# Retention with the centring on ScalarE and the gates on GpSimd, and DeltaNet decay rows spread by a transfer

## The chip, the cores and the metric

The kernel runs on one core of a Trainium2 chip. The metric is the device time in microseconds, from launch to end. All arithmetic is in fp32, or in pairs of fp32r values (a rounded high part and the rest, the low part).

## The reference, cut to what matters

The trunk has two layers over 512 tokens of width 1024. Each layer is a token mixer and an MLP with squared ReLU, both between RMS norms. Layer 0 mixes by retention, layer 1 by gated DeltaNet. What the change touches:

```
def retention(h, w_in, gn_gain, w_out):            # 4 heads, q and k of 256, v of 512 columns
    ...
    scores = q k^T * decay                          # causal, per head
    o = scores v
    mu = mean(o); var = mean((o - mu)^2)            # per token and head, over 512 columns
    o = (o - mu) * rsqrt(var + EPS) * gn_gain
    y = silu(g) * o
    return y @ w_out

def gated_deltanet(...):                            # 8 heads of 128
    ...
    gc = cumsum(g)                                  # per head along the tokens
    decay = where(causal, exp(gc[i] - gc[j]), 0)    # per head and chunk
    lower = where(strict, (k beta) k^T * decay, 0)
    ...
```

The kernel works in chunks of 128 tokens, so DeltaNet has 32 units (8 heads by 4 chunks), each with one triangle of decays, 128 by 128.

## The kernel before, in words

**Engines and streams.** Every engine has its own program, written out by hand, and they meet at counting semaphores. SyncE streams the weights from memory in chunks of 1 MB into two buffers (`w_raw`). ScalarE rounds each chunk to its high part (L940, two instructions), GpSimd subtracts to get the low part (L310, two instructions), and TensorE may use the chunk when `w_ready` says so. A projection is made of parts: one chunk of weights by one of four output tiles, twelve matmuls in three kinds (L417 to L419). A PSUM bank is 128 by 512; there are eight, and a group of parts fills four of them. Banks are released by the semaphore `emptied`.

**Retention** (TensorE L576, VectorE L1545 to L1578, ScalarE L1105 to L1124). TensorE first does the scores of head 0 (L585, 16 instructions in the profile, into banks 0 to 3), then for each head the scores of the next one and then scores by values (L599, 20 instructions in the profile for ten matmuls, into banks 4 to 7). VectorE multiplies the scores by the decay table (L1550); the table is loaded by a transfer that ScalarE issues after its last gate (L1105). TensorE waits for all four decayed tiles of a head at once. For each of the 16 tiles (four heads by four token tiles) VectorE then takes mean and variance (L1566, L1567), subtracts the mean and multiplies by the gate in one instruction that reads the bank (L1570) and releases it, and makes 1/sqrt with one Newton step (L1409 to L1414) from ScalarE's root (L1112). ScalarE scales the tile (L1118). Only behind all that TensorE transposes the first eight tiles (L613, four transposes a tile), ScalarE takes the high parts (L1123) for all tiles, VectorE the low parts (L1577), and the output projection begins (`group` with `RET_OUT`, its first part reads tile 0, 1, 2, 3 of head 0, and it waits for all four at once). The other eight tiles are transposed inside that projection.

**DeltaNet gate rows.** The decays' cumulative sums come from two small matmuls with a triangle of ones and with ones (`sum_g`, L687, L688), for all 32 units as columns. The triangle of decays also needs the sums along the other axis, as a row that all partitions hold. `row_sums` (L695) makes it on TensorE: for each unit, a matmul of the column, broadcast to 128 by 128, with the triangle of ones, into PSUM. `triangles` does this for two heads at a time, together with the products of k with itself (L701), at four places inside the projections of v and q. ScalarE takes the exponential from PSUM with a bias per partition (L1225) into `attn`, GpSimd puts zeros above the diagonal (L366), and VectorE multiplies (L1712), which TensorE waits for before the next pair. At the places around it ScalarE squares k (L1214), starts the convolutions (L1198) and rounds weights, and VectorE convolves (L1670) and makes the columns for k (L1682 on).

Of the kernel before, what the change touches and what calls it, by code (L numbers as in the profile page):

```python
# [79 lines left out]
def hybrid_trunk(nc, x, norm_gains, ret_w_in, ret_gn_gain, ret_w_out, gdn_w_in, gdn_conv_w, gdn_a_log,  # L80
# [42 lines left out]
    bn = plan.tile("bn", [P, RH * TT, 16], F32, act_at + 24 * KB)  # L123
    BN_MEAN, BN_VAR, BN_ROOT, BN_NEWTON, BN_RSTD = 6, 7, 8, 9, 12
# [41 lines left out]
    head_rows = big("head_rows", [P, 4, GH], F32, 99.25)  # L166
    ct = plan.tile("ct", [P, 16, UNITS], F32, dump_at)
# [39 lines left out]
    with ExitStack() as ctx:  # L207
# [94 lines left out]
        def _(pool):  # L302
# [39 lines left out]
            low_parts(4, FIRST_CHUNK[1] - 2)  # L342
# [71 lines left out]
        def _(pe):  # L414
# [161 lines left out]
            def retention():  # L576
                pe.wait_ge(emptied, 4 * RET_OUT[0])
                pe.wait_ge(sem("roped"), KT)

                def scores(h):  # L580
                    if h:
                        pe.wait_ge(sem("decayed"), TT * h)
                    for i in range(TT):
                        for d in range(2):
                            done = pe.matmul(bank[i][:, 0:T - i * P], qk_t[:, KT + 2 * h + d, i * P:(i + 1) * P],  # L585
                                             qk_t[:, 2 * h + d, i * P:T], start=d == 0, stop=d == 1)
                        done.then_inc(sem("scored"), 1)

                scores(0)
                for h in range(RH):  # L590
                    if h + 1 < RH:
                        scores(h + 1)
                    else:
                        pe.wait_ge(sem("decayed"), TT * RH)
# [7 lines left out]
                turn_y(0, 8)  # L602

            def turn_y(first, last):

                for n in range(first, last):
                    h, m = n // TT, n % TT
                    pe.wait_ge(sem("y_scaled"), n + 1)
                    pe.wait_ge(sem("y_gated"), min(n + 9, RH * TT))
# [5 lines left out]
                    done.then_inc(sem("y_transposed"), 1)  # L615

# [66 lines left out]
            def sum_g():  # L683
# [4 lines left out]
                pe.matmul(bank[7][:, UNITS:2 * UNITS], ones, col[:, G, :], start=True, stop=True)\  # L688
                    .then_inc(sem("g_summed"), 1)

            def row_sums(h, b):

                for n in range(TT):
                    g = col[:, G, h * TT + n:h * TT + n + 1].broadcast_to([P, P])
                    done = pe.matmul(bank[b][:, n * P:(n + 1) * P], g, tri, start=True, stop=True)  # L695
                return done
# [15 lines left out]
            def triangles(first):  # L712
# [5 lines left out]
                for i in range(2):  # L718
# [3 lines left out]
                    row_sums(first + i, b).then_inc(sem("tri_rows"), 1)  # L722
# [199 lines left out]
            group(RET_OUT[1], 0, 4, False, y_hi, y_lo, {(0, 1): lambda: turn_y(8, 12), (0, 3): lambda: turn_y(12, 16)},  # L922
                  tiles=(sem("y_low"), 0))
# [10 lines left out]
        def _(act):  # L934
# [173 lines left out]
            splits(RET_OUT, 0, 4, last=1)  # L1108
            for n in range(RH * TT + 1):
                if n < RH * TT:  # L1110
                    act.wait_ge(sem("varied"), n + 1)
                    act.activation(bn[:, n, BN_ROOT:BN_ROOT + 1], bn[:, n, BN_VAR:BN_VAR + 1], ACT.Sqrt, bias=eps)\  # L1112
                        .then_inc(sem("gn_rooted"), 1)
                if n:
                    h, m = (n - 1) // TT, (n - 1) % TT
                    act.wait_ge(sem("gn_inverted"), n)
                    y = gate[:, m, h * RV:(h + 1) * RV]
                    act.activation(y, y, ACT.Copy, scale=bn[:, n - 1, BN_RSTD:BN_RSTD + 1])\  # L1118
                        .then_inc(sem("y_scaled"), 1)
            for n in range(RH * TT):  # L1120
                h, m = n // TT, n % TT
                act.wait_ge(sem("y_transposed"), n + 1)
                act.activation(y_hi[:, 4 * h:4 * h + 4, m * P:(m + 1) * P], tall(y_bank(n)), ACT.Copy)\  # L1123
                    .then_inc(sem("y_high"), 1)  # L1124
# [94 lines left out]
            def tri_exps(first):  # L1219
                for h in (first, first + 1):  # L1220
                    act.wait_ge(sem("tri_rows"), h + 1)
                    b = (0 if h < 4 else 4) + 2 * (h % 2)
                    for n in range(TT):
                        u = h * TT + n
                        done = act.activation(attn[:, u, :], bank[b][:, n * P:(n + 1) * P], ACT.Exp,  # L1225
# [22 lines left out]
            for gi in range(8):  # L1248
# [50 lines left out]
                if gi == 2:  # L1299
                    square_heads(4, GH)  # L1300
# [101 lines left out]
        def _(dve):  # L1402
# [3 lines left out]
            def inv_root(x, root, temp, out_, scale=1.0, add=EPS):  # L1406
# [4 lines left out]
                if x.shape[-1] == 1:  # L1411
                    link(dve.tensor_scalar(t[2], t[0], t[1], t[1], ALU.mult, ALU.mult))
                    link(dve.tensor_scalar(t[2], t[2], -0.5, 1.5, ALU.mult, ALU.add))
# [139 lines left out]
            def inverted(n):  # L1553
                dve.wait_ge(sem("gn_rooted"), n + 1)
                inv_root(bn[:, n, BN_VAR:BN_VAR + 1], bn[:, n, BN_ROOT:BN_ROOT + 1],
                         lambda t: bn[:, n, BN_NEWTON + t:BN_NEWTON + t + 1], bn[:, n, BN_RSTD:BN_RSTD + 1])\
                    .then_inc(sem("gn_inverted"), 1)

            decayed(0)
            for h in range(RH):  # L1560
                if h + 1 < RH:
                    decayed(h + 1)
                for m in range(TT):
                    n = TT * h + m
                    dve.wait_ge(sem("attended"), n + 1)
                    link(dve.bn_stats(bn[:, n, 0:6], bank[4 + m][:, :]))  # L1566
                    dve.bn_aggr(bn[:, n, BN_MEAN:BN_VAR + 1], bn[:, n, 0:6]).then_inc(sem("varied"), 1)  # L1567
                    dve.wait_ge(sem("varied"), n + 1)
                    y = gate[:, m, h * RV:(h + 1) * RV]
                    dve.scalar_tensor_tensor(y, bank[4 + m][:, :], bn[:, n, BN_MEAN:BN_MEAN + 1], y,  # L1570
# [322 lines left out]
```

## Time and profile before

| | |
|---|---|
| median of 3 runs | 1518.33 us (1517.52 to 1521.31) |
| the profiled execution | 1518.14 us |
| its span, first to last instruction | 1516.2 us |
| mean granted TensorE clock | 0.996 of full speed |
| retention, first score matmul to first matmul of the output projection | 285.91 to 347.50 us |
| DeltaNet, where row sums are made | 892.61 to 937.0 us |

The times of instructions in the profile are counted from the span's start. What lies around the span is 1.9 us. An engine's busy time matters only where another engine waits for it; the chain that ended last says which engine the end hangs on.

### The profile page before, as it was taken

To read this page: it belongs to the slowest core of one execution; us is meant where nothing else is said; L and a number is where in the kernel's file an instruction comes from. 1 tells how busy PE (TensorE), PEld (TensorE's weight loads), DVE (VectorE), ACT (ScalarE), POOL (GpSimd) and SP (SyncE) were. 2 spreads that over 40 slices of the span, in tenths; PEclk is the share of its full clock that TensorE was granted. 3 is DMA by queue.
4 is the path that set the end of the run, shared out by engine and by line. 5 is a ranking of instruction groups with operands and counts; after the bars stand their busy time and mean duration, and the time that the engine had idled before them with its cause. 6 is when DMAs were issued, how large, how long until landed. Compare 5 with 4: busy or idle time off the path is not lost.

```text
span 1516.2 us, 19636 instructions
## 1 busy us (share of the span) xinstructions
PE 1471.4 (97%) x7657; PEld 1245.3 (82%) x7657; DVE 607.9 (40%) x1121; ACT 550.7 (36%) x1046; POOL 629.4 (42%) x283
## 2 busy tenths in 40 slices
PE   6999999998999999999999999999998999999997
PEld 6988888657889888888889978889988988888886
DVE  3641002383265410134045544995747540024223
ACT  5232333233253222232234576655735222223231
POOL 5244443302544444444445243355336253534441
PEclk9999999999999999999999999999999999999999
DMA  6222323400333232322323112211023223232321
GB/s 237 102 84 86 108 83 111 139 0 29 98 99 112 84 111 83 96 99 85 110 84 119 56 56 84 84 56 56 15 70 101 81 84 111 83 97 98 111 84 56
DMA packets 66507, 134.22 MB, mean 89 GB/s; under 512 B 3616, under 2 KB 4096, under 8 KB 66176
## 3 DMA queue, kind: packets, MB, share of 16 engines
q1 hardware_dynamic: 64016, 125.90, 25.4%
q10 hardware_dynamic: 2416, 7.27, 1.4%
q8 instruction: 53, 0.87, 0.2%
q14 instruction: 22, 0.18, 0.0%
HBM read 131.06 MB, written 2.10 MB: 88 GB/s over the span
## 4 chain that ended last, share of the span: by engine, by line
PE 88%; DVE 5%; ACT 3%; POOL 2%; DMA 1%; issue 1%; SPq 0%; ACTq 0%; DVEq 0%
PE bank L417 26%; PE bank L418 26%; PE bank L419 26%; PE bank L599 2%; POOL side_lo L310 1%; PE bank L792 1%; PE bank L805 1%; PE bank L585 1%; PE bank L701 1%; ACT squares L1214 1%; DVE mix L1458 1%; DMA w_raw<-in_ret_w_in_dram 1%; DVE act_lo L1484 1%; DVE gv L1670 1%; POOL w_lo L310 1%
## 5 line engine op out<-in xcount | busy, mean ns | idle before, releaser
L310 POOL TENSOR_TENSOR w_lo<-w_raw,w_hi 128x1024 fp32r<-128x1024 f32 (+1 forms) x218 | 520.4, 2410 | 741.0 <-ACT w_hi L940 740.9
L940 ACT ACTIVATE w_hi<-w_raw 128x1024 fp32r<-128x1024 f32 x210 | 211.0, 1055 | 466.7 <-PE bank L419 422.0
L417 PE MATMUL bank<-act_hi,w_hi 128*128 128x512 f32 (+1 forms) x832 | 300.0, 361 | 8.5 <-DVE act_lo L1484 7.3
L418 PE MATMUL bank<-act_lo,w_hi 128*128 128x512 f32 (+1 forms) x832 | 298.3, 359 | 0.0
L419 PE MATMUL bank<-act_hi,w_lo 128*128 128x512 f32 (+1 forms) x832 | 298.3, 359 | 0.0
L418 PE MATMUL bank<-w_lo,hid_hi 128*128 128x512 f32 x480 | 189.0, 394 | 0.0
L417 PE MATMUL bank<-w_hi,hid_hi 128*128 128x512 f32 x480 | 188.2, 392 | 0.0
L419 PE MATMUL bank<-w_hi,hid_lo 128*128 128x512 f32 x480 | 186.4, 388 | 0.0
L417 PEld LDWEIGHTS bank<-act_hi,w_hi 128*128 128x128 f32 x832 | 158.8, 191 | 32.9 <-DVE act_lo L1484 8.8
L1589 DVE TENSOR_TENSOR relu_sq<-relu 128x512 f32<-128x512 f32 x64 | 48.8, 763 | 328.4 <-ACT relu L963 328.1
L419 PEld LDWEIGHTS bank<-act_hi,w_lo 128*128 128x128 f32 x832 | 158.6, 191 | 22.6
L418 PEld LDWEIGHTS bank<-act_lo,w_hi 128*128 128x128 f32 x832 | 158.8, 191 | 21.9
L417 PE MATMUL bank<-w_hi,act_hi 128*128 128x512 f32 x320 | 125.0, 391 | 1.5 <-issue 1.1
L419 PE MATMUL bank<-w_hi,act_lo 128*128 128x512 f32 x320 | 124.5, 389 | 0.0
L418 PE MATMUL bank<-w_lo,act_hi 128*128 128x512 f32 x320 | 124.5, 389 | 0.0
L417 PEld LDWEIGHTS bank<-w_hi,hid_hi 128*128 128x128 f32 x480 | 90.1, 188 | 20.9
L419 PEld LDWEIGHTS bank<-w_hi,hid_lo 128*128 128x128 f32 x480 | 90.1, 188 | 20.2
L418 PEld LDWEIGHTS bank<-w_lo,hid_hi 128*128 128x128 f32 x480 | 90.2, 188 | 18.1
L1540 DVE TENSOR_TENSOR gate<-gate,gains x16 | 16.9, 1072 | 149.8 <-ACT gate L963 149.8
L417 PE MATMUL bank<-act_hi,side_hi 128*128 128x256 f32 x256 | 72.4, 283 | 1.4 <-POOL side_lo L310 1.4
L417 PEld LDWEIGHTS bank<-w_hi,act_hi 128*128 128x128 f32 x320 | 60.1, 188 | 15.0 <-issue 1.9
L418 PE MATMUL bank<-act_lo,side_hi 128*128 128x256 f32 x256 | 71.4, 279 | 0.0
(258 smaller groups left out, 2150.4 us busy)
## 6 DMA issues: line engine op xcount, KB each, us to landing
w_raw<-in_mlp_w_up_dram SPq DMA_DIRECT2D x32, 1024.0 KB, 5.4
w_raw<-in_mlp_w_down_dram SPq DMA_DIRECT2D x32, 1024.0 KB, 5.0
w_raw<-in_ret_w_in_dram SPq DMA_DIRECT2D x24, 1024.0 KB, 5.1
w_raw<-in_gdn_w_in_dram SPq DMA_DIRECT2D x16, 1024.0 KB, 5.3
w_raw<-in_ret_w_out_dram SPq DMA_DIRECT2D x8, 1024.0 KB, 4.9
gains<-in_norm_gains_dram ACTq DMA_DIRECT2D x8, 512.0 KB, 6.1
w_raw<-in_gdn_w_out_dram SPq DMA_DIRECT2D x4, 1024.0 KB, 5.1
resid<-in_x_dram SPq DMA_DIRECT2D x4, 512.0 KB, 9.2
```

The source lines that it names most:

```text
L310: done = nc.gpsimd.tensor_tensor(LO[slot][:, kt, :], w_raw[:, raw, kt, :], HI[slot][:, kt, :].bitcast(F32), ALU.subtract)
L417: pe.matmul(dst, sta_hi, mov_hi, start=first, stop=False)
L418: pe.matmul(dst, sta_hi, mov_lo, start=False, stop=False)
L419: return pe.matmul(dst, sta_lo, mov_hi, start=False, stop=last)
L585: done = pe.matmul(bank[i][:, 0:T - i * P], qk_t[:, KT + 2 * h + d, i * P:(i + 1) * P], qk_t[:, 2 * h + d, i * P:T], start=d == 0, stop=d ...
L599: done = pe.matmul(bank[4 + j][:, :], score[:, h % 2, i, j * P:(j + 1) * P], v_tm[:, i, h * RV:(h + 1) * RV], start=i == 0, stop=i == j)
L701: done = pe.matmul(bank[b][:, n * P:(n + 1) * P], gk[:, h, n * P:(n + 1) * P], other[:, h, n * P:(n + 1) * P], start=True, stop=True)
L792: done = pe.matmul(bank[r][:, n * P:(n + 1) * P], neg_l_t[:, u, :], inv[:, u - batch * UNITS // 2, :], start=True, stop=True)
L805: done = pe.matmul(bank[4 + r][:, n * P:(n + 1) * P], half_prod[:, u - batch * UNITS // 2, :], inv_t[:, u, :], start=True, stop=True)
L940: act.activation(HI[raw if slot is None else slot][:, kt, :], w_raw[:, raw, kt, :], ACT.Copy)\
L1540: dve.tensor_tensor(g, g, gains[:, :, :].rearrange("p a n -> p (a n)")[:, bass.ds(i * GC, GC)], ALU.mult).then_inc(sem("gate_gained"), 1)
L1589: dve.tensor_tensor(relu_sq[:, m, :], relu[:, m, :], relu[:, m, :], ALU.mult)\
```

## The change

**Retention.** `centre` on ScalarE now takes the root, and then reads the bank and writes mean minus value to a new buffer `centred` of three tiles (an Identity activation with scale -1 and the mean as bias); this releases the bank. GpSimd multiplies that tile with the gate (16 multiplications between two loops of low parts). VectorE's instruction L1570 is gone; its Newton step turns the sign. `scale_y` is as before, behind GpSimd. TensorE waits tile by tile for decayed scores, starts the scores of head 0 once banks 0 to 3 are free, transposes tiles 0 to 3 in the middle of head 3 and tiles 4 and 5 behind it, and `first_ret_out` waits for each tile of the low part by itself and transposes the last ten tiles between its parts. ScalarE and VectorE take the first high and low parts before their last tile of statistics.

**DeltaNet.** `row_sums` is gone. `sum_g` has a third matmul that gives the sums with units as rows, 32 by 128. ScalarE copies it to SBUF, sends it to memory (16 KB), waits for that transfer just before it squares the last four heads of k, and issues a second one that reads it back into `attn` for all 128 partitions (2 MB). The exponentials then read and write `attn`.

```diff
@@ tensor, retention
-                pe.wait_ge(emptied, 4 * RET_OUT[0])
+                pe.wait_ge(emptied, 4 * (RET_OUT[0] - 1))
 def scores(h):
-    if h:
-        pe.wait_ge(sem("decayed"), TT * h)
     for i in range(TT):
+        if h:
+            pe.wait_ge(sem("decayed"), TT * (h - 1) + i + 1)
...
     for j in range(TT):
+        pe.wait_ge(sem("decayed"), TT * h + j + 1)
         if h:
-            pe.wait_ge(sem("y_gated"), TT * (h - 1) + j + 1)
+            pe.wait_ge(sem("y_centred"), TT * (h - 1) + j + 1)
...
+        if h == RH - 1 and j == 1:
+            pe.wait_ge(sem("decayed"), TT * RH)
+            turn_y(0, 4)
-turn_y(0, 8)
+turn_y(4, 6)
+def first_ret_out():
+    turns = {(0, 0): (6, 8), (0, 2): (8, 12), (1, 0): (12, 16)}
+    for j in range(4):
+        for m in range(TT):
+            pe.wait_ge(sem("y_low"), TT * j + m + 1)
+            done = part(RET_OUT[1], j, 0, 4, m, False, y_hi, y_lo, fresh=m == 0)
...
@@ gpsimd
-            low_parts(4, FIRST_CHUNK[1] - 2)
+            low_parts(4, RET_OUT[1] + 2)
+            for n in range(RH * TT):
+                pool.wait_ge(sem("y_centred"), n + 1)
+                y = gate[:, m, h * RV:(h + 1) * RV]
+                nc.gpsimd.tensor_tensor(y, y, centred[:, n % 3, :], ALU.mult).then_inc(sem("y_gated"), 1)
+            low_parts(RET_OUT[1] + 2, FIRST_CHUNK[1] - 2)
@@ scalar
+def centre(n):
+    act.wait_ge(sem("varied"), n + 1)
+    act.activation(root <- var, ACT.Sqrt)
+    if n >= 3:
+        act.wait_ge(sem("y_gated"), n - 2)
+    act.activation(centred[:, n % 3, :], bank[4 + n % TT][:, :], ACT.Identity, scale=-1.0,
+                   bias=bn[:, n, BN_MEAN:BN_MEAN + 1]).then_inc(sem("y_centred"), 1)
 for n in range(RH * TT + 1):
     if n < RH * TT:
+        centre(n)
     if n:
+        scale_y(n - 1)
+    if n == RH * TT - 2:
+        high_y(0, 4)
+high_y(4, RH * TT)
@@ vector
     dve.wait_ge(sem("attended"), n + 1)
+    if n == RH * TT - 1:
+        low_y(0, 1)
     link(dve.bn_stats(...)); dve.bn_aggr(...).then_inc(sem("varied"), 1)
-    dve.scalar_tensor_tensor(y, bank[4 + m][:, :], mean, y, ALU.subtract, ALU.mult)
     inverted(n)
+low_y(1, RH * TT)
@@ DeltaNet: tensor
+                pe.matmul(bank[7][0:UNITS, P:2 * P], col[:, G, :], tri, start=True, stop=True)
-                    row_sums(first + i, b).then_inc(sem("tri_rows"), 1)
@@ DeltaNet: scalar, before and in group 2
+  act.activation(g_rows[:, :], bank[7][0:UNITS, P:2 * P], ACT.Copy).then_inc(sem("g_rows_out"), 1)
   act.activation(EXP_G ...); act.activation(EXP_TOT ...)
+  act.wait_ge(sem("g_rows_out"), 1)
+  act.dma_start(g_spread, g_rows[:, :]).then_inc(sem("g_kept"), 16)
   act.wait_ge(sem("rest_made"), 1); act.activation(ct[:, 8, :] ...)
+  act.wait_ge(sem("g_kept"), 16)
+  act.dma_start(attn as 128 x 4096, g_spread broadcast to 128 partitions).then_inc(sem("g_spread"), 16)
   square_heads(4, GH)
@@ tri_exps
-  act.wait_ge(sem("tri_rows"), h + 1)
+  act.wait_ge(sem("g_spread"), 16)
-  act.activation(attn[:, u, :], bank[b][:, n * P:(n + 1) * P], ACT.Exp, bias=...)
+  act.activation(attn[:, u, :], attn[:, u, :], ACT.Exp, bias=...)
```

## Rows read from the trace of the kernel before

**Rows 1.** The page, part 4: the chain that ended last, by engine.

```profile
PE 88%; DVE 5%; ACT 3%; POOL 2%; DMA 1%; issue 1%; SPq 0%; ACTq 0%; DVEq 0%
```

**Rows 2.** Timeline of TensorE, retention: start, us, line, count [idle before, releaser].

```profile
285.91 4.58 PE L585 MATMUL bank<-qk_t 128*128 128x512 f32 x16 [0.78 <-ACT gate L963]
292.16 4.58 PE L585 MATMUL bank<-qk_t 128*128 128x512 f32 x16 [1.67 <-DVE score L1550]
...
347.50 0.80 PE L417 MATMUL bank<-w_hi,y_hi 128*128 128x512 f32 x1 [3.91 <-DVE y_lo L1577]
...
354.53 1.91 PE L613 MATMUL bank<-square,gate 128*128 128x128 f32 x16
...
361.79 1.91 PE L613 MATMUL bank<-square,gate 128*128 128x128 f32 x16
```

**Rows 3.** Busy time by window (us, engines, granted clock PEclk), start of output projection.

```profile
347.50:350.70 3.20, 3.20 (x8) 2.55 (x9) 2.34 (x4) 0.84 (x2) 0.00 (x0) 0.52 0.00 0
```

**Rows 4.** The chain that ended last in order of time, retention: start, us, what.

```profile
285.41 4.94 DMA decay<-in_decay_dram
290.43 1.70 DVE score L1550 x4
...
322.55 8.60 PE bank L599 x20
...
354.69 1.75 PE bank L613 x16
```

**Rows 5.** Timeline of VectorE, one of the 16 retention tiles and the next.

```profile
325.94 0.69 DVE L1566 BATCH_NORM_STATS2 bn<-bank 128x6 f32<-128x512 f32 x1
...
326.88 0.75 DVE L1570 SCALAR_TENSOR_TENSOR gate<-bank,bn,gate 128x512 f32<-128x512 f32 x1
...
328.43 0.69 DVE L1566 BATCH_NORM_STATS2 bn<-bank 128x6 f32<-128x512 f32 x1
```

**Rows 6.** Timeline of ScalarE, retention.

```profile
289.67 1.28 ACT L1112 ACT_TABLE_LOAD   x1
...
344.35 3.99 ACT L1123 ACTIVATE y_hi<-bank 128x512 fp32r<-128x512 f32 x8
```

**Rows 7.** Instructions that touch gains, GpSimd: duration in ns, min/median/max.

```profile
L337 POOL TENSOR_TENSOR normed<-resid,gains x8: 1272/1314/1321, 6.5 to 1139.8; 128x512 f32<-128x512 f32 x8
```

**Rows 8.** Timeline of TensorE, DeltaNet projections.

```profile
884.32 0.47 PE L417 MATMUL bank<-act_hi,w_hi 128*128 128x512 f32 x1 [0.75 <-issue]
...
892.61 1.05 PE L695 MATMUL bank<-square,col 128*128 128x128 f32 x8
...
905.28 1.16 PE L695 MATMUL bank<-square,col 128*128 128x128 f32 x8 [0.69 <-DVE neg_l_t L1712]
...
954.40 1.97 PE L651 MATMUL bank<-square,gv 128*128 128x128 f32 x16
```

**Rows 9.** The chain that ended last, DeltaNet: row sums of one head.

```profile
922.75 0.89 PE bank L695 x8
```

**Rows 10.** Timeline of ScalarE, DeltaNet.

```profile
876.97 0.23 ACT L1296 ACTIVATE ct<-ct 128x32 f32<-128x32 f32 x1 [0.54 <-DVEq L1679]
879.55 0.28 ACT L1214 ACTIVATE squares<-bank 128x128 bf16<-128x128 f32 x1 [2.35 <-PE bank L651]
...
894.15 0.23 ACT L1318 ACTIVATE ct<-ct 128x32 f32<-128x32 f32 x1 [6.17 <-DVEq L1685]
```

**Rows 11.** Timelines of GpSimd and of VectorE, DeltaNet.

```profile
895.40 4.75 POOL L310 TENSOR_TENSOR w_lo<-w_raw,w_hi 128x1024 fp32r<-128x1024 f32 x2 [16.68 <-ACT w_hi L940]
...
945.35 8.99 DVE L1670 SCALAR_TENSOR_TENSOR gq<-bank,conv_w,gq 128x509 f32<-128x509 f32 x12 [5.04 <-ACT gq L1198]
```

**Rows 12.** DMA issues: count, KB each, us from issue to landing.

```profile
out_dram<-resid SPq DMA_DIRECT2D x8, 256.0 KB, 2.0
gains<-in_ret_gn_gain_dram ACTq DMA_DIRECT2D x1, 1024.0 KB, 4.6
...
head_rows<-in_gdn_dt_bias_dram ACTq DMA_DIRECT2D x1, 4.0 KB, 4.9
```

More of the change, by code:

```diff
@@ L615, in turn_y @@
                     done.then_inc(sem("y_transposed"), 1)
+            def first_ret_out():
[4 more added lines that the diff above has]
+                        done = part(RET_OUT[1], j, 0, 4, m, False, y_hi, y_lo, fresh=m == 0)
+                        if j == 3:
+                            done.then_inc(bank_full, 1)
+                        elif m == 3:
+                            done.then_inc(chunk_used, 1)
+                        if (j, m) in turns:
+                            turn_y(*turns[j, m])
             def mlp(layer):
@@ L687, in sum_g @@
                 pe.matmul(bank[7][:, 0:UNITS], tri, col[:, G, :], start=True, stop=True)
-                pe.matmul(bank[7][:, UNITS:2 * UNITS], ones, col[:, G, :], start=True, stop=True)\
+                pe.matmul(bank[7][:, UNITS:2 * UNITS], ones, col[:, G, :], start=True, stop=True)
+                pe.matmul(bank[7][0:UNITS, P:2 * P], col[:, G, :], tri, start=True, stop=True)\
                     .then_inc(sem("g_summed"), 1)
[L691 to L696, printed above, removed]
             def products(h, b, other):
@@ L920, in _ @@
             retention()
-            group(RET_OUT[1], 0, 4, False, y_hi, y_lo, {(0, 1): lambda: turn_y(8, 12), (0, 3): lambda: turn_y(12, 16)},
-                  tiles=(sem("y_low"), 0))
+            first_ret_out()
             tail(1, RET_OUT, y_hi, y_lo)
@@ new lines, in scale_y, with high_y @@
+            def scale_y(n):
+                h, m = n // TT, n % TT
+                act.wait_ge(sem("gn_inverted"), n + 1)
+                act.wait_ge(sem("y_gated"), n + 1)
+                y = gate[:, m, h * RV:(h + 1) * RV]
+                act.activation(y, y, ACT.Copy, scale=bn[:, n, BN_RSTD:BN_RSTD + 1]).then_inc(sem("y_scaled"), 1)
+            def high_y(first, last):
+                for n in range(first, last):
+                    h, m = n // TT, n % TT
+                    act.wait_ge(sem("y_transposed"), n + 1)
+                    act.activation(y_hi[:, 4 * h:4 * h + 4, m * P:(m + 1) * P], tall(y_bank(n)), ACT.Copy)\
+                        .then_inc(sem("y_high"), 1)
@@ L1118, in _ @@
[L1118 to L1124, printed above, removed]
+                    scale_y(n - 1)
+                if n == RH * TT - 2:
+                    high_y(0, 4)
@@ L1220, in tri_exps @@
                 for h in (first, first + 1):
[L1221 to L1222 removed]
+                    act.wait_ge(sem("g_spread"), 16)
                     for n in range(TT):
                         u = h * TT + n
[L1225 removed]
+                        done = act.activation(attn[:, u, :], attn[:, u, :], ACT.Exp,
                                               bias=col[:, NEG_GCUM, u:u + 1])
@@ L1404, in _, with inv_root @@
             link = chain.link
-            def inv_root(x, root, temp, out_, scale=1.0, add=EPS):
+            def inv_root(x, root, temp, out_, scale=1.0, add=EPS, sign=1):
                 t = [temp(n) for n in range(3)]
@@ L1555, in inverted, with low_y @@
                 inv_root(bn[:, n, BN_VAR:BN_VAR + 1], bn[:, n, BN_ROOT:BN_ROOT + 1],
-                         lambda t: bn[:, n, BN_NEWTON + t:BN_NEWTON + t + 1], bn[:, n, BN_RSTD:BN_RSTD + 1])\
+                         lambda t: bn[:, n, BN_NEWTON + t:BN_NEWTON + t + 1], bn[:, n, BN_RSTD:BN_RSTD + 1], sign=-1)\
                     .then_inc(sem("gn_inverted"), 1)
+            def low_y(first, last):
+                for n in range(first, last):
+                    h, m = n // TT, n % TT
+                    dve.wait_ge(sem("y_high"), n + 1)
+                    where = (slice(None), slice(4 * h, 4 * h + 4), slice(m * P, (m + 1) * P))
+                    dve.tensor_tensor(y_lo[where], tall(y_bank(n)), y_hi[where].bitcast(F32), ALU.subtract)\
+                        .then_inc(sem("y_low"), 1)
             decayed(0)
```

32 lines of the change are left out of this document (12 added, 20 removed).

## The prediction

> **What bounds the kernel now.** I read the chain that ended last first. TensorE carries 88% of it [rows 1], so a microsecond is won only where TensorE idles, runs at the low clock, or does work that goes away. I then went along TensorE's timeline through the two stages that the change touches and, at each idle stretch, to the timeline of the engine that ended it.
>
> In retention TensorE idles three times. The first idle is 0.78 us ahead of the first scores; the second is 1.67 us, ended by decayed scores at 292.16 [rows 2]. These hang on a transfer: the decay table is issued at 285.41, takes 4.94 us, and VectorE starts at 290.43 and needs 1.70 us for four tiles, for all of which TensorE waits [rows 4]. From there to the last matmul of head 3 TensorE is full: heads 2 and 3 begin at 322.55 and take 8.60 us each [rows 4], to 339.75. VectorE however needs 2.49 us a tile (325.94 to 328.43 [rows 5]), and ends its sixteenth late; behind it come scaling, high parts and low parts. So the third idle stretch: eight tiles of transposes (twice the 1.75 us of 16 [rows 4]) would end at 343.25, and the output projection starts at 347.50 [rows 2]. It also starts slowly: in the window that begins there the granted clock is 0.52, that is 1.2 of 2.4 GHz [rows 3], after an idle stretch of 3.91 us. The first two parts take 354.53 - 347.50 = 7.03 us, where the next two take 361.79 - 354.53 - 1.75 = 5.51 us [rows 2, 4].
>
> In the DeltaNet projections TensorE is nearly full, with 0.75 us idle at 884.32 and 0.69 us at 905.28 [rows 8]. A second chain runs beside it, close behind: squares of k from 879.55, convolution, the root at 894.15 for which ScalarE had waited 6.17 us [rows 10], the weight rounding behind that in ScalarE's queue, and GpSimd's low part from 895.40 to 900.15 [rows 11].
>
> **Retention, step by step.** Starting the scores of head 0 earlier (up to 0.78 us) is worth nothing: TensorE then waits for the decay table that much longer, and the table's issue is not moved. Waiting per tile is worth something: the first decayed tile is 512 wide and comes some 0.7 us (an estimate from the 0.69 us that a 512-wide read of a bank takes VectorE [rows 5]) after 290.43, so TensorE resumes at 291.1 and not at 292.16: **1.0 us**. The three later tiles are there before TensorE asks.
>
> VectorE loses 0.75 us a tile [rows 5], but then waits for ScalarE's root, which that instruction had covered, so I take 2.2 us a tile. Four tiles and four decayed tiles are then some 10.6 us a head against TensorE's 12.9 (8.60 and about 4.3 for scores [rows 2, 4]). ScalarE gets 16 centrings: about 0.5 us each, as the eight reads of a bank in 3.99 us [rows 6]; with root and scaling some 1.4 us a tile. GpSimd gets 16 products of 1.3 us [rows 7]. It has nothing else there, since its low parts of the first two output chunks are put ahead. Neither is near the 3.2 us a tile that TensorE takes (12.9 / 4). A bank is asked for one head after it was filled, so the longer way to its release costs nothing. That cover is four to nine microseconds wide at each tile; if it were gone, each late tile would cost what it is late.
>
> At the end: head 3 starts at 331.15 - 1.0 = 330.1. Its parts of 1, 2, 3 and 4 matmuls (0.86 us each) with four tiles of transposes (1.75 us) after the second end at 331.0, 332.7, 337.1 and 340.5; two more tiles of transposes end at 341.4. The first low part is made at 340.5 + 0.7 = 341.2, because VectorE does it before its last statistics and ScalarE took its high part by about 340. So the output projection can start at once, with 0.2 us to spare. The last tile's way is statistics 342.1, centring 343.0, product 344.3, scaling 345.0; the banks for tiles 6 and 7 are wanted at 344.2 (centring of tile 15 done at 343.0), the low parts of the second head at 350.5 (there by about 348). The third chunk of output weights is rounded behind the last high part on ScalarE, so it moves forward with TensorE; before and after it is ready some 4 us ahead. So the wait of 347.50 - 343.25 = **4.2 us** goes, and with it the slow start, 7.03 - 5.51 = **1.5 us**. The transposes are only moved. Retention: 1.0 + 4.2 + 1.5 = **6.7 us**. What is next late is the first low part; if it comes 1 us later, 1 us of this is lost. I bound the stage from 3 us (it starts idle, with half of the slow start left) to 7.5 us (the first idle goes too).
>
> **DeltaNet, step by step.** Each head's row sums take 0.89 us on TensorE [rows 9], in eight heads 7.1 us. The added matmul has the same width as one of the four units in such a row: 0.2 us. Not all of this lies on the path:
> - The first pair (892.61 [rows 8]) is worth nothing. TensorE gets to the next weight chunk 1.8 us earlier, but its low part is ready at 900.15 whatever TensorE does [rows 11], and the next products wait for the masked triangles of the first pair, whose exponentials ScalarE reaches in its queue only behind the rounding, not behind TensorE. The idle 0.69 us at 905.28 [rows 8] grows instead.
> - The second pair comes at that place and is worth its 1.8 us, since what is behind it is TensorE's own work.
> - The third and fourth are worth 3.6 us. ScalarE does not wait for row sums there any more, so VectorE's triangles, the diagonal and the next convolution begin some 6 us earlier. Before, that convolution ran from 945.35 to 954.34 [rows 11] and TensorE's transposes at 954.40 [rows 8] came right behind it. After, I have it end at 948.4 and TensorE there at 949.3.
> - The 0.2 us of the added matmul shift the squares and with them the whole chain.
>
> So 1.8 + 3.6 - 0.2 = **5.2 us**. I take 5.1, for the slightly longer way through the copy.
>
> **The two transfers.** ScalarE issues the store at about 876.7, after the copy (0.2 us). The nearest rows are the stores at the end, 2.0 us for 256 KB, and the smallest load, 4.9 us for 4 KB issued amid others [rows 12]. I take 2.0, because it is a store on idle queues. Landing at 878.7 and 0.4 us of issue end at 879.1, inside the 2.35 us that ScalarE idles before 879.55 [rows 10]. Cover gone (4.9 us), the squares start at 882.0, **2.2 us** late, and all behind them. The lower end is nothing, not a gain, as the idle stretch hangs on TensorE. Behind the waiting instruction stand the squares, for which TensorE waits (884.32 [rows 8]). The spread of 2 MB: 1 MB broadcast took 4.6 us [rows 12], so some 7 to 10 us with a weight chunk beside it, landing by 889. It is wanted by ScalarE at 901, the weight chunk at 894.15.
>
> The Trainium skill (DMA: Bandwidth & Descriptors, Anatomy of one DMA) gives about 2.0 us fixed and bytes at 436 GB/s, and warns that the receipt of a write can be surprisingly long when the target is HBM. By its fit the store would take 2.0 us and the spread 6.8 us, as in my sum; by its warning it speaks for the rival below.
>
> **Sum.** 6.7 + 5.1 = 11.8 us from the profiled execution's 1518.14 us (span 1516.2 and 1.9 around it): **1506.3 us**. The median of the runs is 1518.33, so the two agree to 0.2 us.
>
> **Rivals.**
> - *The store is slow* (12%). For it: the 4.9 us row. Against it: the 2.0 us rows and empty queues. 2.2 us lost: 1508.5.
> - *The second chain sets DeltaNet* (10%). For it: the idle stretches at 884.32 and 905.28. Against it: its later waits went through the row sums themselves. TensorE then waits for the 5.1 us that it no longer works: 1511.4.
> - *The start of the output projection stays late* (8%). For it: only 0.2 us to spare, and three engines in a row. It costs 3.7 us: 1510.
> - *Table loads take the place of the wait* (4%), the slower side. ScalarE's table load takes 1.28 us [rows 6]. One load served all roots and copies before, but no row shows an Identity. If it needed another table than the root, each tile would have two loads, 2.56 us, so about 3.9 us a tile against TensorE's 3.2. Counted from 298, the fifteenth ends at 356.5 and the projection starts at 357.8, 10.3 us later than before; less 5.1 of DeltaNet that is 1523.3. It decides from 3.2 us a tile, and turns the sum to a loss from about 3.6.
> - Anything else, either way (6%).
>
> The Trainium skill (ScalarE: Activation LUTs, Table sets) says that copy and identity are in every set. By it the last rival has no loads; the case's rows show it for copy alone.
>
> **Chances.** Forecast 60%, with a range of its own of 1504.5 to 1508. The range reaches down to 1502.5 (the upper bound of retention, 7.5, and all 7 us of row sums come to 14.5, less what I can't rule out) and up to 1511.5, which takes in the three faster rivals and leaves out table loads and half of the rest. A measurement here can tell about 0.3%, 4.6 us. All cases but the table loads and part of the rest are faster by more than that: 0.91 faster, 0.05 within, 0.04 slower.
>
> **What would show it.** Right: no TensorE idle between 291 and the end of the first output group; granted clock 1.00 at its start; one table load in the stage; group of the output projection starting at 341 to 342; TensorE idle growing to about 1 us before the second pair of products and no other new one; turning of v at 949 less 6.7, that is near 942.6 on the new time scale; a store of 2 us. Wrong: ScalarE waiting over 2.5 us before the squares of the fifth head, TensorE idle ahead of the output projection, or the exponentials waiting for the spread.

## The result, and the profile after

The changed kernel takes 1505.62 us (median of 4 runs, 1504.56 to 1506.10) against 1517.92 (4 runs beside it, 1517.42 to 1521.31): ratio 0.9915, 95% interval 0.9903 to 0.9928, 12.3 us less. 1506.3 had been forecast. One further execution of the kernel before, beside later runs, took 3017.77 us and is left out of every comparison.

The page, part 4 (by engine), answers [rows 1]:

```profile
PE 90%; DVE 4%; ACT 2%; POOL 1%; DMA 1%; issue 1%; SPq 0%; ACTq 0%; DVEq 0%
```

The timeline of TensorE in retention answers [rows 2] (start, us, engine, line, count, idle before and releaser). Scores are now L594, scores by values L608, transposes L626, the projection L426:

```profile
283.77 4.48 PE L594 MATMUL bank<-qk_t 128*128 128x512 f32 x16
289.98 4.58 PE L594 MATMUL bank<-qk_t 128*128 128x512 f32 x16 [1.74 <-DVE score L1592]
...
331.36 1.91 PE L626 MATMUL bank<-square,gate 128*128 128x128 f32 x16
333.11 6.17 PE L608 MATMUL bank<-v_tm,score 128*128 128x512 f32 x14
339.12 1.04 PE L626 MATMUL bank<-square,gate 128*128 128x128 f32 x8
340.07 0.51 PE L426 MATMUL bank<-w_hi,y_hi 128*128 128x512 f32 x1
342.95 1.03 PE L626 MATMUL bank<-square,gate 128*128 128x128 f32 x8
```

The first idle stretch is gone and the second has grown into its place: 1.74 us, ended by the first decayed tile. From 289.98 to the end of the projection there is none. The projection starts at 340.07 and its first part takes its 2.9 us at once, at full clock (busy time by window, the last columns being granted clock, DMA share and GB/s; it answers [rows 3]):

```profile
340.07:343.40 3.33, 3.33 (x18) 2.76 (x18) 2.83 (x10) 1.86 (x5) 1.31 (x1) 1.00 0.00 0
```

The chain that ended last, in order of time, at the second scores, answers [rows 4]; one tile of 0.70 us is waited for where it was four:

```profile
284.20 4.95 DMA decay<-in_decay_dram
...
289.24 0.70 DVE score L1592
...
289.98 4.58 PE bank L594 x16
```

One retention tile on VectorE (two starts of its statistics), ScalarE and GpSimd, and ScalarE's table load (timelines; these answer [rows 5 to 7]):

```profile
288.46 1.28 ACT L1131 ACT_TABLE_LOAD   x1
...
323.43 0.69 DVE L1619 BATCH_NORM_STATS2 bn<-bank 128x6 f32<-128x512 f32 x1
...
325.58 0.69 DVE L1619 BATCH_NORM_STATS2 bn<-bank 128x6 f32<-128x512 f32 x1
...
324.57 0.67 ACT L1135 ACTIVATE centred<-bank,bn 128x512 f32<-128x512 f32 x1
...
325.31 1.27 POOL L350 TENSOR_TENSOR gate<-gate,centred 128x512 f32<-128x512 f32 x1 [0.89 <-ACT centred L1135]
```

VectorE takes 2.15 us a tile (323.43 to 325.58) where it took 2.49; the centring takes ScalarE 0.67 us and the product GpSimd 1.27, both beside it. There is one table load in the stage, so Identity shares the root's table. The Trainium skill (ScalarE: Activation LUTs, Table sets) says that identity is in every set, and the trace agrees (one load, 1.28 us). VectorE at the end of head 3: the first low part, then the last statistics:

```profile
339.32 0.69 DVE L1607 TENSOR_TENSOR y_lo<-bank,y_hi 128x512 fp32r<-128x512 f32 x1 [1.18 <-ACT y_hi L1151]
339.93 0.69 DVE L1619 BATCH_NORM_STATS2 bn<-bank 128x6 f32<-128x512 f32 x1
```

The low part ends at 340.01, and the projection starts at 340.07: the narrow place is narrower than forecast (0.06 us to spare and not 0.2), and holds.

In DeltaNet, TensorE (answers [rows 8]; L678 transposes, which is called turning below, the products of k are L722, the added matmul L716):

```profile
859.11 1.91 PE L678 MATMUL bank<-square,gk 128*128 128x128 f32 x16
...
865.08 0.41 PE L716 MATMUL bank<-square,col 128*32 128x128 f32 x2
865.41 0.50 PE L426 MATMUL bank<-act_hi,w_hi 128*128 128x512 f32 x1
...
886.08 1.16 PE L722 MATMUL bank<-gk 128*128 128x128 f32 x8 [0.37 <-DVE gv L1714]
...
892.25 0.50 PE L426 MATMUL bank<-act_hi,w_hi 128*128 128x512 f32 x1 [0.69 <-POOL w_lo L313]
897.59 2.05 PE L722 MATMUL bank<-gk 128*128 128x128 f32 x16 [0.96 <-DVE neg_l_t L1756]
...
941.22 1.91 PE L678 MATMUL bank<-square,gv 128*128 128x128 f32 x16
```

The idle stretches of 0.37 us (ahead of the second products of the first pair) and 0.69 us (at the low part of the next weight chunk) are new: they take up 1.06 us of the first pair's removed 1.8. The third, 0.96 us ahead of the second pair, is the 0.69 us of the kernel before [rows 8], grown by 0.27. From 897.59 to the turning of v at 941.22 there is none. ScalarE (answers [rows 10]): both transfers are issued without holding it up, and the squares wait for TensorE as before:

```profile
866.62 0.34 ACTq L1333 DMA_DIRECT2D g_spread<-g_rows  x1
...
868.74 0.34 ACTq L1340 DMA_DIRECT2D attn<-g_spread  x1
871.62 0.28 ACT L1251 ACTIVATE squares<-bank 128x128 bf16<-128x128 f32 x1 [2.66 <-PE bank L678]
...
893.15 2.45 ACT L1261 ACTIVATE attn<-attn,col 128x128 f32<-128x128 f32 x8
```

The same eight exponentials, read from PSUM, in the kernel before:

```profile
901.10 2.18 ACT L1225 ACTIVATE attn<-bank,col 128x128 f32<-128x128 f32 x8
```

The store landed in 1.4 us and the spread in 7.8 (answers [rows 12]), over 16 us before the exponentials.

**Where the time went.** Profiled executions differ in where retention begins, by 1.7 us among these kernels (the decay table is issued between 283.81 and 285.54), so stretches between marks are compared, not clock readings. Marks: the issue of the decay table; the start of the scores of head 1 (the second scores); the first transposes of the norm behind retention; the first turning of k; the turning of v. The medians come from several groups of runs, in which the kernel before took 1517.9 to 1519.4 us, so medians of different groups compare only to some 1.5 us.

| kernel | issue to 2nd scores | issue to norm | k to v | median us |
|---|---|---|---|---|
| before | 6.75 | 149.54 | 86.91 | 1517.92 |
| changed | 5.78 | 142.83 | 82.11 | 1505.62 |
| retention alone | 5.78 | 142.82 | 86.95 | 1510.62 |
| DeltaNet alone | 6.86 | 149.68 | 82.14 | 1513.88 |
| waits only | 5.57 | 148.52 | 86.91 | 1517.25 |
| late turns | 5.81 | 148.14 | 82.13 | 1512.89 |
| four stores | 5.76 | 142.78 | 87.02 | 1510.11 |
| first pair kept | 5.78 | 142.83 | 82.11 | 1506.24 |
| last pairs kept | 5.80 | 142.85 | 85.73 | 1510.39 |
| root behind | 5.82 | 142.84 | 80.31 | 1504.82 |
| order only | 5.89 | 144.64 | 82.14 | 1506.34 |
| root behind, first pair kept | 5.62 | 142.67 | 80.86 | 1504.56 |
| decay early | | 140.81 | 82.14 | 1504.83 |
| both early | | 140.77 | 80.27 | 1501.79 |

(With the decay table early the scores of heads 0 and 1 run as one piece, so the first column is empty.)

Retention gives 149.54 - 142.83 = 6.71 us; DeltaNet 86.91 - 82.11 = 4.80 up to the turning of v, and 5.22 up to the joining of the inverses, the matmuls that put the inverted triangles together (from the first turning of k at 867.49 to 1027.49 before, 859.11 to 1013.89 after). The last 0.42 us are no steady part of the gain. From the turning of v to the joining the kernel before takes 73.09 us, and of the eleven executions with the changed DeltaNet six take 73.0 and five 72.7. Where it is 73.0, TensorE idles some 0.4 us at a low part on the way; where it is 72.7, as in the changed kernel, that stretch is missing. The kernel before has it:

```profile
997.78 0.50 PE L417 MATMUL bank<-w_hi,act_hi 128*128 128x512 f32 x1 [0.41 <-POOL w_lo L310]
```

The profiled pair differs by 13.4 us in its spans: 6.71 and 5.22, 1.2 ahead of the issue of the decay table, where kernels that are equal up to there differ as much, and 0.3 elsewhere. So 11.5 to 11.9 us are traced to the change, and the medians say 12.3.

### The profile page after: what moved, and what is told of

It is laid out like the page before. It is cut to its first block, busy times and chain, and to the rows that moved or that the text cites. A ratio compares the mean times of both kernels' runs of the same rounds, so it can differ in the third digit from the quotient of the medians.

```text
span 1502.8 us, 19558 instructions
## 1 busy us (share of the span) xinstructions
PE 1461.3 (97%) x7595; PEld 1235.9 (82%) x7595; DVE 598.6 (40%) x1105; ACT 560.5 (37%) x1063; POOL 649.2 (43%) x299
## 4 chain that ended last, share of the span: by engine, by line
PE 90%; DVE 4%; ACT 2%; POOL 1%; DMA 1%; issue 1%; SPq 0%; ACTq 0%; DVEq 0%
PE bank L426 27%; PE bank L427 27%; PE bank L428 26%; PE bank L608 2%; POOL side_lo L313 1%; PE bank L812 1%; PE bank L825 1%; PE bank L678 1%; PE bank L594 1%; PE bank L722 1%; DVE mix L1500 1%; DMA w_raw<-in_ret_w_in_dram 1%; DVE act_lo L1526 1%; DVE gv L1714 1%; PE bank L473 1%
## 5 line engine op out<-in xcount | busy, mean ns | idle before, releaser
L426 PE MATMUL bank<-act_hi,w_hi 128*128 128x512 f32 (+1 forms) x832 | 299.7, 360 | 9.8 <-DVE act_lo L1526 7.9
L426 PE MATMUL bank<-w_hi,hid_hi 128*128 128x512 f32 x480 | 188.2, 392 | 0.0
L426 PEld LDWEIGHTS bank<-act_hi,w_hi 128*128 128x128 f32 x832 | 158.3, 190 | 34.8 <-DVE act_lo L1526 9.2
L426 PE MATMUL bank<-w_hi,act_hi 128*128 128x512 f32 x320 | 124.9, 390 | 1.0 <-issue 1.0
L426 PEld LDWEIGHTS bank<-w_hi,hid_hi 128*128 128x128 f32 x480 | 90.1, 188 | 20.9
L426 PE MATMUL bank<-act_hi,side_hi 128*128 128x256 f32 x256 | 72.3, 282 | 1.4 <-POOL side_lo L313 1.4
L982 ACT ACTIVATE relu<-bank 128x512 f32<-128x512 f32 x64 | 38.0, 597 | 91.2 <-PE bank L428 91.2
L426 PEld LDWEIGHTS bank<-w_hi,act_hi 128*128 128x128 f32 x320 | 60.1, 188 | 14.3 <-issue 1.8
```

The source lines that it names most:

```text
L426: pe.matmul(dst, sta_hi, mov_hi, start=first, stop=False)
L982: act.activation(dst, bank[4 * p + m][:, :], func).then_inc(emptied, 1)
```

## The experiments

**Retention alone and DeltaNet alone.** The hunks of the one part on the kernel before.

> The retention part of the change alone, DeltaNet as before. My theory: it is worth 6.7 us by itself (from 1517.9 to about 1511.2), all of it won before the second part of the output projection. Rival: the two parts are not independent, and the whole 12.3 us needs both; then this one moves by 4 us or less or by 9 us or more.

> The DeltaNet part alone, retention as before. Theory: 4.8 to 5.1 us (to about 1513.0), though 7.1 us of row sums are gone: none from the first pair of heads. Rival (the second chain of ScalarE and VectorE sets the stage): under 1 us, 1517. Rival (all row sums were on the path): 6.9 us, 1511.0.

Measured: 1510.62 us, ratio 0.9945 (0.9929 to 0.9962), and 1513.88 us, ratio 0.9968 (0.9956 to 0.9981). The medians say 7.6 and 4.3 us against 1518.20 beside them, the stretches 6.72 and 4.77: independent, and they sum to the whole (11.5 us by the stretches, 11.9 by these medians).

**Waits only.**

```diff
 def scores(h):
-    if h:
-        pe.wait_ge(sem("decayed"), TT * h)
     for i in range(TT):
+        if h:
+            pe.wait_ge(sem("decayed"), TT * (h - 1) + i + 1)
```

The per-tile wait ahead of scores by values, and the early start of the first scores, are in it too.

> The kernel before with only TensorE's waits per decayed tile and the early start of the scores; centring, gates, transposes as before. Theory: the scores of head 1 start 1.0 to 1.1 us earlier and everything moves by that: 1516.9. The earlier scores of head 0 (0.78 us) are lost in the wait for the decay table: TensorE idles 1.7 us ahead of the second scores still. Rival: both idle stretches are won, 2.4 us, 1515.5. Rival: VectorE, which was nearly full, takes it back, 1517.9.

Measured: 1517.25 us, ratio 0.9991 (0.9982 to 1.0001), too little for the total to tell. The stretch from the issue of the table to the norm is 1.02 us shorter, and TensorE idles 1.53 us ahead of the second scores (timeline of TensorE):

```profile
289.56 4.58 PE L585 MATMUL bank<-qk_t 128*128 128x512 f32 x16 [1.53 <-DVE score L1550]
...
344.89 0.50 PE L417 MATMUL bank<-w_hi,y_hi 128*128 128x512 f32 x1 [3.92 <-DVE y_lo L1577]
```

The wait ahead of the projection is unmoved, 3.92 us.

**Late turns.**

```diff
-                        if h == RH - 1 and j == 1:
...
-                            turn_y(0, 4)
-                turn_y(4, 6)
+                turn_y(0, 8)
...
-            first_ret_out()
+            group(RET_OUT[1], 0, 4, False, y_hi, y_lo, {(0, 1): turn_y(8, 12), (0, 3): turn_y(12, 16)}, ...)
```

High and low parts are taken behind the last tile again, as before.

> The changed kernel, with the transposes and the start of the output projection in the old order (eight tiles of transposes behind the last head, all four low parts waited for, high and low parts behind the last tile). Centring on ScalarE and gates on GpSimd stay. Theory: the wait for the first low parts hangs on the order, not on VectorE's load: the way of the last tile over ScalarE and GpSimd is as long as VectorE's lag was, so TensorE idles some 3.6 us and starts at the low clock again: 5.1 us slower than the changed kernel, 1510.7. Rival: the 0.75 us a tile off VectorE brought most of the gain, then at most 2 us slower, 1507.6.

Measured: 1512.89 us, ratio to the kernel before 0.9964 (0.9951 to 0.9976), 7.3 us over the changed kernel's median. The stage is 5.31 us longer than the changed one; this is the effect of the edit. Another 1.6 us of the profiled execution come from the clock at the joining of the inverses (below), where nothing was edited; whether the other executions had this is not shown. TensorE idles 3.62 us and then has 0.57 of its clock (timeline, and busy time by window):

```profile
344.36 0.50 PE L426 MATMUL bank<-w_hi,y_hi 128*128 128x512 f32 x1 [3.62 <-DVE y_lo L1604]
```

```profile
344.30:348.10 3.80, 3.74 (x10) 2.94 (x11) 2.40 (x5) 0.90 (x2) 0.00 (x0) 0.57 0.00 0
```

With VectorE's load taken off and the old order, nearly all of the gain at that place is gone: 148.14 us to the norm, against 148.52 with the waits alone. That raised the reverse question.

**Order only.** Centring and gates back on VectorE (and TensorE's waits for a free bank back on `y_gated`):

```diff
-                act.activation(centred[:, n % 3, :], bank[4 + n % TT][:, :], ACT.Identity, scale=-1.0, ...)
...
-                nc.gpsimd.tensor_tensor(y, y, centred[:, n % 3, :], ALU.mult).then_inc(sem("y_gated"), 1)
+                    dve.scalar_tensor_tensor(y, bank[4 + m][:, :], mean, y,
+                                             ALU.subtract, ALU.mult).then_inc(sem("y_gated"), 1)
```

> The changed kernel with the centring and the gates back on VectorE in one instruction, as in the kernel before (nothing on GpSimd, only the root and the scaling on ScalarE). The new order stays: waits per tile, transposes in the middle of head 3, first high and low part ahead of the last tile, output projection tile by tile; DeltaNet as changed. Theory, formed after the late turns came out 5.3 us slower in the stage: the order alone brings the gain. VectorE ends the fifteenth tile some 0.7 us before the last bank is filled, so the first low part is late by 0.3 us at most: within 0.5 us of the changed kernel, 1505.6 to 1506.1. Rival: VectorE's 2.49 us a tile are needed back, it lags at the end as before, and at least 2.5 us of the 6.7 go: 1508.1 or more.

Measured: 1506.34 us, ratio 0.9925 (0.9907 to 0.9944), 0.7 us over the changed kernel's median. The stretch is 1.81 us longer, and the timeline shows where: the second scores take 6.28 us and not 4.58, at a granted clock of 0.56, behind an idle stretch of 1.85 us (1.74 in the changed kernel, where the clock stayed at 1.00). That the edit caused this is not shown. From the third scores on it is the same, 305.07 to 429.12 us (124.05) against 302.99 to 427.03 (124.04), with no idle ahead of the projection:

```profile
290.37 6.28 PE L588 MATMUL bank<-qk_t 128*128 128x512 f32 x16 [1.85 <-DVE score L1582]
...
341.20 1.04 PE L620 MATMUL bank<-square,gate 128*128 128x128 f32 x8
342.15 0.51 PE L420 MATMUL bank<-w_hi,y_hi 128*128 128x512 f32 x1
```

```profile
290.30:293.90 3.60, 3.53 (x5) 1.59 (x6) 1.04 (x5) 0.00 (x0) 2.20 (x1) 0.56 0.77 227
```

So moving the centring to ScalarE and the gates to GpSimd gives nothing that this kernel shows; the new order gives all. VectorE ends the fifteenth tile in time (it idles 0.29 us behind it), and the low part of the first is taken before the sixteenth in either. Apart from the wait for each decayed tile, which was run alone above, the new order has several parts: the transposes in the middle of head 3, the high and low parts ahead of the last tile, and a wait for each low part by itself. Which of them are needed was not tested.

**Four stores.**

```diff
+                    for again in range(1, 4):
+                        act.wait_ge(sem("g_kept"), 16 * again)
+                        act.dma_start(g_spread, g_rows[:, :]).then_inc(sem("g_kept"), 16)
-                    act.wait_ge(sem("g_kept"), 16)
+                    act.wait_ge(sem("g_kept"), 64)
```

> The changed kernel with three more stores of the same 16 KB, each waited for before the next, ahead of the spread. In the changed kernel a store lands in 1.4 us, the spread is issued at 868.74 and the squares of k start at 871.62, so 2.5 us (2.88 less the 0.34 us of issue) are free there. Theory: the wait lies in ScalarE's idle time and is paid only beyond it: three more stores of about 1.5 us move the issue to 873.2, the squares to 873.6, 2.0 us late, and the turning of v by as much: 1507.6. Rival: the waits are on the path in full, 4.5 us later, 1510.1. Rival: the squares are not on the path, no change, 1505.6.

Measured: 1510.11 us (2 runs), ratio 0.9942 (0.992 to 0.9963). ScalarE:

```profile
869.00 3.13 ACTq L1341 DMA_DIRECT2D g_spread<-g_rows  x3
876.35 0.34 ACTq L1343 DMA_DIRECT2D attn<-g_spread  x1
876.75 0.28 ACT L1251 ACTIVATE squares<-bank 128x128 bf16<-128x128 f32 x1 [7.53 <-DMA g_spread<-g_rows]
```

Three more stores took 7.35 us and not 4.5: the last was issued by 871.8 (869.00 + 3.13 less 0.34 of issue), behind a weight chunk of 1 MB issued at 870.75, and landed some 4.5 us later. The one before it, issued at about 870.4 and so just ahead of the chunk, still took 1.4. Of the 7.35 us the 2.5 free ones are hidden, and 4.9 reach the turning of v (87.02 against 82.11). So the size of my theory failed by the price of a store, and its total fell on the rival's by chance; that idle time hides the wait, and that the squares are on the path, stand. It also gives the change's risk a number, from one case: the same 16 KB cost 1.4 us on idle queues and once some 4.5 behind a weight chunk (that the chunk is the cause is argued from the times of issue), and in the changed kernel the chunk is issued 3.9 us behind the store.

**First pair kept, last pairs kept.** The row sums computed again for heads 0 and 1, or 4 to 7, with no reader:

```diff
+                    if first == 0:        # or: first >= 4
+                        row_sums(first + i, b)
                     products(first + i, b + 1, gk)
```

> The changed kernel with the row sums of the first two heads computed again (1.8 us of TensorE's work, nobody reads them). Theory: the first pair is worth nothing, since TensorE waits behind it for the low part of the next weight chunk and for the masked triangles; 1505.6, TensorE's idle stretch of 0.69 us at that low part and the 0.37 us ahead of the second products gone, the stretch from the first turning of k to the turning of v 82.1 us as before. Rival (each microsecond of TensorE's work counts): 1507.4.

> The changed kernel with the row sums of the last four heads computed again (3.6 us of TensorE's work, nobody reads them). Theory: these lie on the path in full, 3.6 us slower, 1509.2; the stretch from the first turning of k to the turning of v is 85.7 us. Rival (ScalarE and VectorE set this stage): under 1 us, 1506.4.

Measured: 1506.24 us, 0.9918 (0.9900 to 0.9936), and 1510.39 us, 0.9943 (0.9925 to 0.9960). The stretch from k to v is 82.11, to the hundredth that of the changed kernel, and 85.73, which is 3.62 more. (The median of the second is 4.8 us higher; its profiled execution has the low clock at the joining, of which below.) Of TensorE in the first:

```profile
887.79 1.06 PE L728 MATMUL bank<-gk 128*128 128x128 f32 x8
888.60 0.48 PE L426 MATMUL bank<-act_hi,w_hi 128*128 128x512 f32 x1
892.80 0.41 PE L426 MATMUL bank<-act_hi,w_hi 128*128 128x512 f32 x1
898.05 2.05 PE L728 MATMUL bank<-gk 128*128 128x128 f32 x16 [0.98 <-DVE neg_l_t L1764]
```

The idle 0.37 and 0.69 us are filled, and the 0.98 stays (0.96 in the changed kernel). That is 1.06 us of the 1.78 us put back; the other 0.7 lie in no idle stretch that the profile names.

**Root behind, and with the first pair kept.**

```diff
+                if gi == 3:                      # behind the rounding of group 3
+                    act.wait_ge(sem("kq_x_made"), 1)
+                    act.activation(ct[:, 2, :], ct[:, 0, :], ACT.Sqrt).then_inc(sem("kq_rooted"), 1)
...
-                if gi == 2:                      # end of group 2
-                    act.wait_ge(sem("kq_x_made"), 1)
-                    act.activation(ct[:, 2, :], ct[:, 0, :], ACT.Sqrt).then_inc(sem("kq_rooted"), 1)
```

> The changed kernel, and ScalarE takes the root for the columns of k behind the rounding of the next weight chunk and not ahead of it. In the changed kernel ScalarE idles 6.17 us for VectorE there, rounds behind it, and GpSimd's low part is late by 0.69 us, blocks two VectorE column instructions (2.29 and 2.31 us) and the exponentials come 2 us later; TensorE idles 0.37, 0.69 and 0.96 us. Theory: with the rounding ahead, the low part is ready some 6 us earlier and the masked triangles some 2 to 4 us earlier, so 0.69 and 0.96 us go: 1.6 us faster, 1504.0, and the first pair's row sums have then paid. Rival: the squares, the convolution and the products' bank set that place anyway: no change.

> The kernel with the root behind the rounding, and the row sums of the first two heads computed again. Theory: with the low part early the place is no longer bound by it, so TensorE's 1.8 us count here, where they cost nothing in the changed kernel: the stretch from the first turning of k to the turning of v is 82.1 us, not the 80.3 of the kernel with the root behind; 1506.6. Rival: the first pair is hidden here as well, 80.3 us, 1504.8.

Measured: 1504.82 us, 0.9905 (0.9887 to 0.9923), stretch 80.31, 1.80 less; and 1504.56 us (2 runs), 0.9911 (0.9891 to 0.9931), stretch 80.86. The totals of the two lie too close to tell them apart; the stretches do. GpSimd's low part starts 20.7 us behind the first turning of k, where it was 28.4, and VectorE's two column instructions that ran beside it take 0.19 us each and not 2.29 and 2.31. GpSimd and TensorE with the root behind:

```profile
881.69 4.77 POOL L313 TENSOR_TENSOR w_lo<-w_raw,w_hi 128x1024 fp32r<-128x1024 f32 x2 [9.48 <-ACT w_hi L959]
...
888.01 1.16 PE L722 MATMUL bank<-gk 128*128 128x128 f32 x8 [0.37 <-DVE gv L1714]
...
897.62 2.05 PE L722 MATMUL bank<-gk 128*128 128x128 f32 x16 [0.25 <-DVE neg_l_t L1756]
```

The first theory holds: the rounding in ScalarE's queue bound the place (1.80 us by the stretch, 1.6 expected). The second does not: with the low part early, the first pair's 1.8 us cost only 0.55. Row sums fill the 0.37 us in which TensorE waits for VectorE's convolution to release a bank and the 0.25 us for the masked triangles. These account for half of the 1.2 us that are hidden; where the rest goes is not shown.

**Decay early, both early.** The table of head 0 is loaded into `decay_0` (the place of `dump`) at the start; VectorE waits for the large table only at head 1.

```diff
+    decay_0 = plan.tile("decay_0", [P, T], F32, dump_at)
...
+            act.dma_start(decay_0[:, :], decay_c[:, 0, :]).then_inc(sem("decay_0_landed"), 16)
```

> The changed kernel, with the decay table of head 0 loaded a second time at the start into a buffer that is free until then. Theory: TensorE's 1.74 us idle ahead of the scores of head 1 hang on the table's transfer alone, and with it the early start of the scores pays too: no idle there, 1.7 us faster, 1503.9. Rival: VectorE, which has the last gate products before it, or the banks hold it up in the same place: under 0.5 us.

> Both: the root behind the rounding, and the decay table of head 0 early. Theory: two places of TensorE's own path, so the sum, 1.8 + 1.7 = 3.5 us faster than the changed kernel, 1502.1, and 16 us faster than the kernel before. Rival: one of them is given back at the next wait, 1503.9.

Measured: 1504.83 us, 0.9912 (0.9895 to 0.9929), and 1501.79 us (4 runs, 1500.19 to 1504.06), 0.9896 (0.9878 to 0.9914). In the first all 32 score instructions of heads 0 and 1 run without a pause, and the stretch to the norm is 2.02 us shorter, the 1.74 and the restart:

```profile
284.00 8.79 PE L595 MATMUL bank<-qk_t 128*128 128x512 f32 x32
```

Its total is only 0.8 us lower. The profiled execution has the low clock at the joining; whether the other three had it, and what else keeps the total up, is not shown. With both, 1.84 us less from k to v and 2.06 to the norm, 3.9 by the stretches and 3.8 by the medians: 16.4 us less than the kernel before beside it. (Its four runs spread over 3.9 us, so the medians' 3.8 is a rough number.) This is the best version run.

## Why the prediction was right, and where it was not

- *The decay wait, 1.0 us.* 0.97 measured, and the early scores of head 0 gave nothing, as forecast (1.74 us idle in their place). Loading the table early shows what held them.
- *The late start of the projection, 4.2 us, and the slow clock, 1.5.* 6.71 less 0.97 is 5.74, forecast 5.7. But the cause that I put first, that VectorE needs 2.49 us a tile and so ends late, was not what had to be mended: with VectorE as loaded as before, the order alone won the same. What counted was that everything stood behind the sixteenth tile, though it was wanted for the first. I had bounded VectorE's time per tile and worked out its new end; I did not work out its old load under the new order, which would have shown this (fifteenth tile done before the last bank is filled).
- *0.2 us to spare at the first low part.* It was there 0.06 us ahead of TensorE's start. The start itself, 340.07, is 341.3 on the scale of the kernel before (retention begins 1.2 us earlier in this execution), inside the forecast 341 to 342.
- *DeltaNet.* The split in pairs was right: 0, 1.8 and 3.6 forecast, 0.00 and 3.62 measured for first and last. The second was not put back by itself; by subtraction, 4.80 + 0.3 of the added matmul leaves 1.5 for it. Two terms were off in size. The added matmul takes 0.33 us (865.08 to 865.41), not 0.2. The exponentials from SBUF take 2.45 us for eight, where the same form from PSUM took 2.18 (901.10 before), which I had put at no cost. The wait ahead of the second pair grew by the same 0.27 us (0.69 to 0.96), and the second pair falls short of 1.8 by as much; that the one causes the other was not tested. I had also forecast no new idle stretch but that one, grown to 1 us; there are two, 0.37 and 0.69, and the first of them hangs on VectorE's convolution, which the forecast did not name. Up to the joining the stage gave 5.22, forecast 5.1, but that closeness is in part luck: 4.80 of it is steady, and 0.42 comes and goes with the idle stretch at the low part. So the stretches traced give 6.7 + 4.8 = 11.5, forecast 11.8.
- *The transfers.* The store landed in 1.4 us (2.0 forecast), the spread in 7.8 (7 to 10). Neither cost anything. The fit of the Trainium skill (DMA: Bandwidth & Descriptors, Anatomy of one DMA), which is for transfers issued from GpSimd, gives 2.0 and 6.8 as estimates; these were issued from ScalarE, and the measurements decide: below it for the small store, above it for the spread, beside which a weight chunk was loaded. The Trainium skill's warning there, that the wait for a write to be confirmed can be surprisingly long when it goes to HBM, did not come true on idle queues (1.4 us).
- *The rivals.* Slow store: not in this kernel, and 4.9 us late when three more stores were put in. The second chain: it sets the first pair's place and no more. Late first low part: no. Table loads: no.

## What to carry to other kernels

When the last stage starts late behind an engine that looks full, ask first which tile is wanted first and what stands ahead of it in the queues; unloading the engine may give nothing. Work taken off the bounding engine pays only where the next thing it wants is there already: look for what is ready at a fixed time (a rounding behind another engine's wait, a table that was loaded late), and keep the removed work in one place at a time to see which part pays. Compare stretches between marks, not totals, when an edit is worth about 1 us, and look whether the stretch differs between executions of kernels that are equal there.

## What the runs showed that I had not expected

In these executions an idle stretch of TensorE of only some 2 us is sometimes followed by the low clock. At the joining of the inverses TensorE idles 1.84 to 2.28 us in all 14 profiled executions; in five of them the next 4 us have a granted clock of 0.57 to 0.63, that is 1.2 GHz for most of it, and the stretch to the next norm is 115.9 us and not 114.2 to 114.5: some 1.6 us. The same fell on the second scores in one execution, behind 1.85 us of idle, where those of the others that idle there kept 1.00 behind 1.53 to 1.78. The length of the idle stretch does not decide it: both outcomes are seen at 1.84 and at 2.22. Retention alone and the changed kernel (timelines, joining):

```profile
1020.07 5.44 PE L817 MATMUL bank<-inv,neg_l_t 128*128 128x128 f32 x32 [1.84 <-issue]
```

```profile
1013.89 3.81 PE L812 MATMUL bank<-inv,neg_l_t 128*128 128x128 f32 x32 [2.22 <-issue]
```

It accounts for 1.6 us between profiled executions of edits that are themselves worth 1 to 2 us. How often it falls in the other executions, and so what it does to the medians, is not shown. What decides between the two outcomes stays open.
